# A two-layer encoder step: norms after w_out taken chunk by chunk, GpSimd scaling one chunk, and four seams between stages re-ordered

## The reference

```
mod = silu(c) @ w_ada + b_ada            # six vectors: shift, scale, gate, twice
h = rms_norm(x, g_pre_mix) * (1 + sc1) + sh1
q_s, k_s, v_s, q_f, k_f, v_f, f = split(h @ w_in)
o = concat(window_attention(rope(q_s), rope(k_s), v_s, sinks),
           forgetting_attention(q_f, k_f, v_f, cumsum(log_sigmoid(f))))
x = x + gt1 * rms_norm(o @ w_out, g_post_mix)
h = rms_norm(x, g_pre_mlp) * (1 + sc2) + sh2
u = square(relu(h @ w_up))               # 4096 wide
x = x + gt2 * rms_norm(u @ w_down, g_post_mlp)
```

## Time and profile before

| | |
|---|---|
| profiled execution, device time | 2996.36 us |
| its span of work | 2994.0 us |
| TensorE busy | 2778.9 us (93%) |
| VectorE busy | 1207.7 us (40%) |
| ScalarE busy | 893.3 us (30%) |
| GpSimd busy | 80.3 us (3%) |
| chain that ended last | TensorE 85%, VectorE 7%, ScalarE 3%, transfers 3%, issue 2% |

### The profile page before, as it was taken

The page is one execution under the profiler, slowest core; times in us unless marked ns, Lnnn a source line. Parts: engine busy times, 40 slices in busy tenths (PEclk is TensorE's granted clock), DMA queues, the critical chain, the costliest instruction groups (busy, mean ns, idle before and its releaser), DMA issues.

```text
span 2994.0 us, 45563 instructions
## 1 busy us (share of the span) xinstructions
PE 2778.9 (93%) x18807; PEld 2543.2 (85%) x18807; DVE 1207.7 (40%) x2117; ACT 893.3 (30%) x1711; POOL 80.3 (3%) x50
## 2 busy tenths in 40 slices
PE   4999889896999999999969988999969999999997
PEld 3999666594999999999859985766959999999996
DVE  3214747307433333333450257561183333333335
ACT  4222747324221111221231236562241122111222
POOL 0000300000000000000000003000000000000000
PEclk7999989797999999999979999898979999999998
DMA  8110621221111111111341116121211111111121
GB/s 282 49 64 19 200 65 38 72 87 72 57 42 42 42 56 42 42 42 43 139 153 57 47 59 205 30 57 39 106 68 56 42 42 42 56 42 42 42 78 67
DMA packets 158367, 211.48 MB, mean 71 GB/s; under 512 B 8864, under 2 KB 131792, under 8 KB 157712
## 3 DMA queue, kind: packets, MB, share of 16 engines
q1 hardware_dynamic: 158240, 209.66, 21.1%
HBM read 170.45 MB, written 31.00 MB: 67 GB/s over the span
## 4 chain that ended last, share of the span: by engine, by line
PE 85%; DVE 7%; ACT 3%; DMA 3%; issue 2%; SPq 0%; ACTq 0%; DVEq 0%
PE ps L1385 24%; PE ps L1387 23%; PE ps L1386 23%; PE ps L1678 2%; DVE th L1013 1%; PE ps L1431 1%; PE ps L1630 1%; PE ps L1660 1%; PE ps L1438 1%; DVE st L1196 1%; DMA raw<-w_in 1%; DMA ada_w<-w_ada 1%; PE ps L1573 1%; PE ps L1631 1%; DVE xr L1035 1%
## 5 line engine op out<-in xcount | busy, mean ns | idle before, releaser
L1385 PE MATMUL ps<-hh,wh 128*128 128x352 f32 x2304 | 760.8, 330 | 49.6 <-DVE hl L1021 34.1
L1387 PE MATMUL ps<-hh,wl 128*128 128x352 f32 x2304 | 750.6, 326 | 0.0
L1386 PE MATMUL ps<-hl,wh 128*128 128x352 f32 x2304 | 749.2, 325 | 0.0
L1385 PE MATMUL ps<-uh,wh 128*128 128x352 f32 x1536 | 500.2, 326 | 1.4 <-ACT r_t L934 1.4
L1386 PE MATMUL ps<-ul,wh 128*128 128x352 f32 x1536 | 493.7, 321 | 0.0
L1387 PE MATMUL ps<-uh,wl 128*128 128x352 f32 x1536 | 493.5, 321 | 0.0
L1385 PEld LDWEIGHTS ps<-hh,wh 128*128 128x128 f32 x2304 | 440.7, 191 | 57.4 <-issue 30.5
L1386 PEld LDWEIGHTS ps<-hl,wh 128*128 128x128 f32 x2304 | 442.4, 192 | 0.4
L1387 PEld LDWEIGHTS ps<-hh,wl 128*128 128x128 f32 x2304 | 440.7, 191 | 0.0
L1363 DVE TENSOR_TENSOR y<-ps,y 128x352 f32<-128x352 f32 x384 | 198.1, 523 | 426.3 <-PE ps L1387 426.2
L557 ACT ACTIVATE wh<-raw 128x2048 fp32r<-128x2048 f32 (+1 forms) x90 | 172.0, 1912 | 585.6 <-PE ps L1780 573.7
(11 more groups left out here) (231 smaller groups left out, 3010.8 us busy)
## 6 DMA issues: line engine op xcount, KB each, us to landing
ada_v<-w_ada SPq DMA_DIRECT2D x32, 1024.0 KB, 5.3
raw<-w_up SPq DMA_DIRECT2D x32, 1024.0 KB, 5.3
raw<-w_down SPq DMA_DIRECT2D x32, 1024.0 KB, 4.8
x_kept<-xr SPq DMA_DIRECT2D x12, 1408.0 KB, 8.9
ada_w<-w_ada SPq DMA_DIRECT2D x16, 1024.0 KB, 9.1
...
```

The costliest lines, as they stand in the source:

```text
L1385: pe.matmul(out, w_hi, m_hi, start=start and k == 0, stop=False)
L1386: pe.matmul(out, w_hi, m_lo, start=False, stop=False)
L1387: return pe.matmul(out, w_lo, m_hi, start=False, stop=stop and k == nk - 1)
```

## The change

The same sums are computed, some with their factors in another order. What changes is the order of the lists and who does what, at four places of each layer.

*Norms and MLP.* The norm's work on a chunk is cut from its place behind w_out and set among the groups of round 1 and of the first MLP step, which is written out apart from the loop over the other steps (`first`). A chunk now goes through scale, add, square, factor and affine step before the next begins, and the first MLP step takes its w_up groups chunk by chunk, four per chunk. `pre_rms` and `pre_affine` become `scaled` (x times coefficient times factor, one pass) and a second pass on two engines: ScalarE adds the shift and rounds (`affine_hi`), VectorE adds it and subtracts the rounded half (`affine_lo`). The result goes to a buffer of its own, `tn`. `mean` and `mean_of_parts` stand between the 12th and 13th matmul of a group, or behind one. GpSimd scales chunk 1 of y in place of VectorE, and its fill of y comes after the last `affine_lo`.

*Forgetting attention's beginning.* The last two window steps come ahead of the first two scores groups, the 64 small matmuls of `mod_columns` are set in eights before the scores of x = 0 to 7, and SyncE loads the first score rows one weight block earlier.

*w_out's beginning.* `new_scores` is ahead of w_out and goes over the four heads of a set in turn, its transposes and products one group earlier; ScalarE and VectorE split the first weights earlier.

*In-projection.* VectorE's split of the next weights goes behind the next unit's first rope, and the first block of window queries is rounded within the last unit, into a buffer of its own (`sqh0`).

The diff, cut to its core. GpSimd and SyncE, and the table of the norms' order:

```diff
+                cs = slice(CH, 2 * CH)
+                pool.wait_ge(sm("rb_ok"), idx + 1)
+                pool.tensor_tensor(y[:, :, cs], y[:, :, cs], rb[idx % 2][:, None, :].broadcast_to([P, KT, CH]), ALU.mult).then_inc(sm("y_pool"), 1)
...
-                    if b == 13:
+                    if b == 12:
...
+        NORMS = [(NPRE1, 0), (NPRE1, 1), (NPRE1, 2), (NPOST1, 0), (NPRE2, 0), (NPOST1, 1), (NPOST1, 2), (NPRE2, 1), (NPRE2, 2),
+                 (NPOST2, 0), (NPOST2, 1), (NPOST2, 2)]
```

ScalarE:

```diff
+            def affine_hi(l, c):
...
+                    for k in range(4 * hf, 4 * hf + 4):
+                        for (c0, c1, s_) in stream_pieces(c):
+                            ins = act.activation(hh[:, k, c0:c1], tn[:, k, c0:c1], ACT.Identity, bias=mod[:, 24 + k, s_:s_ + 1])
+                    ins.then_inc(sm("h_hi"), 1)
...
+                        if u == N_TM - 1 and i == 6:
+                            q_hi(0)
...
-                    if w == 15:
-                        expo(0)
+                expo(0)
...
+                    if x == 65:
...
                         split_hi(l, W_WO0)
+                        new_evac()
...
-                split_hi(l, W_WO0 + 1)
...
+                                split_hi(l, W_WO0 + 1)
...
+                        if r == 1 and q == 7:
+                            pre_sq(l, NPRE2, 0)
...
-                        if r == 1 and q % 4 == 3:
-                            post_sq(l, NPOST1, c, l * 24 + 12)
...
+                        if r == 1:
+                            if q in (3, 7):
+                                post_sq(l, NPOST1, c, l * 24 + 12)
+                            if q == 4:
+                                norm_rb(l, NPOST1, 0)
+                            if q == 7:
+                                norm_rb(l, NPRE2, 0)
+                            if q == 8:
+                                affine_hi(l, 0)
+                                norm_rb(l, NPOST1, 1)
+                            if q == 9:
+                                split_hi(l, W_MLP0)
...
-                    split(1)
+                    if not first:
+                        split(1)
...
+                        if first and q == 4:
+                            affine_hi(l, 2)
...
+                            if q == 0:
+                                pre_sq(l, NPRE2, 1)
+                                norm_rb(l, NPOST1, 2)
+                            if q == 1:
+                                norm_rb(l, NPRE2, 1)
+                            if q == 2:
+                                affine_hi(l, 1)
+                            if q == 3:
+                                pre_sq(l, NPRE2, 2)
+                                norm_rb(l, NPRE2, 2)
```

VectorE:

```diff
+            def scaled(l, c):
...
+                            ins = dve.scalar_tensor_tensor(out=tn[:, k, c0:c1], in0=xr[:, k, c0:c1], scalar=coef[:, 2, k, s_:s_ + 1],
+                                                           in1=rb[idx % 2][:, c0 - c * CH:c1 - c * CH], op0=ALU.mult, op1=ALU.mult)
+                    ins.then_inc(sm("nt_ok" if hf else "h_full"), 1)
...
+            def affine_lo(l, c):
...
+                dve.wait_ge(sm(f"x_saved{c}"), (l * 2 + 2) * 16)
...
+                    for k in range(4 * hf, 4 * hf + 4):
+                        for (c0, c1, s_) in stream_pieces(c):
+                            ins = dve.scalar_tensor_tensor(out=hl[:, k, c0:c1], in0=tn[:, k, c0:c1], scalar=mod[:, 24 + k, s_:s_ + 1],
+                                                           in1=hh[:, k, c0:c1].bitcast(F32), op0=ALU.add, op1=ALU.subtract)
...
+                ins.then_inc(sm("h_ok"), 1)
...
+                if by_pool:
+                    dve.wait_ge(sm("y_pool"), 2 * l + 1)
...
-                    if ends(q) and n_of(it) + 2 < W_WO0:
+                    if ends(q) and u < U_GATE and n_of(it) + 2 < W_WO0:
                         split_lo(l, n_of(it) + 2)
+                    if u > U_GATE and i == 0 and n_of(it) + 1 < W_WO0:
+                        split_lo(l, n_of(it) + 1)
...
+                    if u == N_TM - 1 and i == 7:
+                        q_lo(0)
...
+                    if x == 66:
+                        split_lo(l, W_WO0)
...
-                    if x == 69:
-                        split_lo(l, W_WO0)
...
-                split_lo(l, W_WO0 + 1)
...
+                split_lo(l, W_WO0 + 1)
...
-                post_norm(l, NPOST1, 0)
-                post_norm(l, NPOST1, 1)
-                post_norm(l, NPOST1, 2)
-                pre_rms(l, NPRE2, 0)
-                pre_affine(l, NPRE2, 0)
+                post_scale(l, NPOST1, 0)
+                post_add(l, NPOST1, 0)
+                scaled(l, 0)
+                affine_lo(l, 0)
                 split_lo(l, W_MLP0)
-                pre_lo(l, NPRE2, 0)
-                pre_rms(l, NPRE2, 1)
...
+                            if q == 0:
+                                post_scale(l, NPOST1, 2)
+                            if q == 1:
+                                scaled(l, 1)
+                            if q == 2:
+                                affine_lo(l, 1)
+                            if q == 3:
+                                post_add(l, NPOST1, 2)
...
+                        if first and q == 3:
+                            scaled(l, 2)
+                            affine_lo(l, 2)
```

TensorE:

```diff
+                s_tail(15)
+                s_tail(16)
                 scores(0)
-                s_tail(15)
                 scores(1)
-                s_tail(16)
-                pe.wait_ge(sm("so_lo"), (l + 1) * 16)
-                for b in range(16):
-                    ins = mod_columns(ps[:, 7, 4 * b:4 * b + 4], mrow[b // 8][:, (b % 8) * 256:(b % 8 + 1) * 256])
-                ins.then_inc(sm("mod_mm"), 1)
...
+                        outs = [ps[32 * hd:32 * hd + 32, A_BANK[w], 0:W] for hd in range(4)]
...
+                        for h, out in zip(heads, outs):
...
+                            ins = pe.matmul(out, aqs[r, (0 if w < 2 else 4) + h // 2, :], kst[r, w, :] if w < 2 else kft[r, h // 2, :],
...
+                        if w >= 2:
+                            for h, out in zip(heads, outs):
+                                pe.matmul(out, ident[0:NH_F, h:h + 1].broadcast_to([NH_F, NEW]), fsn[:, :], start=False, stop=False,
+                                          skip_group_check=True)
...
+                    if x < 8:
+                        if x == 0:
+                            pe.wait_ge(sm("so_lo"), (l + 1) * 16)
+                        for b in (2 * x, 2 * x + 1):
+                            ins = mod_columns(ps[:, 7, 4 * b:4 * b + 4], mrow[b // 8][:, (b % 8) * 256:(b % 8 + 1) * 256])
+                        if x == 7:
+                            ins.then_inc(sm("mod_mm"), 1)
...
+                new_scores()
...
+                            if r == 1 and k == 4:
+                                if q == 5:
+                                    mean_of_parts(l, NPOST1, 0)
+                                if q == 8:
+                                    mean(l, NPRE2, 0)
+                                if q == 9:
+                                    mean(l, NPOST1, 1)
...
-                                new_scores()
+                            if 1 <= q < 5:
+                                new_transposes(q - 1)
...
-                free_slots(7, 2)
-                mean(l, NPOST1, 2)
-                mean_of_parts(l, NPOST1, 2)
-                for c in range(NCH):
-                    mean(l, NPRE2, c)
-                    mean_of_parts(l, NPRE2, c)
...
+                        if r == 1:
+                            if q == 4:
+                                mean(l, NPOST1, 0)
+                            if q == 8:
+                                mean_of_parts(l, NPRE2, 0)
+                            if q == 9:
+                                free_slots(7)
+                                mean_of_parts(l, NPOST1, 1)
+                            if q == 11:
+                                free_slots(7)
...
+                        if q in ((0, 2) if first else (0, 6)):
...
+                        if first and q % 4 == 0:
                             pe.wait_ge(sm("h_ok"), l * 6 + 4 + c)
...
+                                if q == 1:
+                                    mean(l, NPOST1, 2)
+                                if q == 2:
+                                    mean_of_parts(l, NPRE2, 1)
+                                if q == 5:
+                                    mean(l, NPRE2, 2)
                             ins = step(W_MLP0 + b, ps[:, q % 4, 0:CH], b, j, slice(c * CH, (c + 1) * CH), k, KT, hh, hl)
...
+                        if first:
+                            if q == 1:
+                                mean_of_parts(l, NPOST1, 2)
+                                mean(l, NPRE2, 1)
+                            if q == 5:
+                                mean_of_parts(l, NPRE2, 2)
```

274 lines of the change are left out of this document (147 added, 127 removed).

## The result

The changed kernel takes 2879.41 us (median of four runs, 2872.48 to 2886.38) against 2996.07: a ratio of 0.9613 with a 95% interval of 0.9581 to 0.9645. Forecast were 2891, between 2855 and 2940. The four runs are two pairs, 2885.58 and 2886.38, and 2873.24 and 2872.48, with a granted clock of 0.964 to 0.965 and of 0.969; what makes the pairs is the first thing the experiments ask. So 2879 lies between two groups, and no execution took it. The profiled execution is the 2885.58 one, with a span of 2883.8.

The account below looks back on a forecast made before the run. TensorE, busy 93% of the span, was taken as the bound, so gains come from its gaps or low clock. A 4.8, B 11.8, C 17.1 and D 18.3 make 52.0 a layer, 104 for two: 2891 us, range 2855 to 2940.

Parts of the forecast that it names:

- A: In-projection: two TensorE waits shrink, 2.8 for a rope and 2.0 for window queries; 4.8 us gained per layer.
- B: Beginning of the forgetting attention: waits and the spreading block go, some cost returns; 11.8 us per layer, bounds 0.5 and 18.
- in the midst of big matmuls I count them at full clock: Forgetting attention's beginning: spreading matmuls set among big ones cost 0.40 a block, 16 x 0.40 = 6.4 us.
- Rival (1): The clock stays up at the seams: B 16, C 24, D 21, with A 65.8 per layer; 2864 us, chance 0.20.
- C: Beginning of w_out: earlier weight split and new_scores ahead of w_out; 17.1 us gained per layer, bounds 4 and 24.
- one group earlier I count 1.0: In w_out: the sample's products, waited for behind group 8, come one group earlier and gain 1.0 us.
- Rival (2): The heads of new_scores don't overlap in this form, so C is 3.6; 2918 us, chance 0.13.
- D: Norms between w_out and the MLP: 126.8 us becomes 108.5, with four waits left; 18.3 gained per layer, bounds 8 and 24.
- GpSimd has some 3 to spare: Norms, chunk 1: GpSimd's scale takes 5.2 us, leaving some 3 before TensorE takes the mean behind group u1.
- the 0.7 put down for the collision: Norms: 0.7 us lost because GpSimd and VectorE take turns, around the split of the MLP's first weights.
- Rival (3): GpSimd's scale beside a busy VectorE takes three times as long, 16 us, costing 7.4 a layer; 2906 us, chance 0.15.
- rival (5): Slower: small matmuls put into groups bring the clock to 1.2 GHz over the stretch, and it stays; 3014 us, chance 0.02.

Follow-up runs that it names:

- no_mod: The changed kernel with 15 of the 16 blocks of spreading matmuls (mod_columns) left out; 2867.83 us.
- heads_serial: The changed kernel with new_scores going head by head, each head's four matmuls in a row, as before the change; 2934.47 us in one execution.
- combined: The changed kernel with four edits: sample's copies before w_out's split, VectorE scaling the second chunk, one sum of parts moved, affine_lo reporting half chunks; 2852.97 us.

## Why the prediction was right, step by step

- **A** (4.8): 4.9 in layer 0, with 2.8 and 2.0 for the two waits. Right. In layer 1 the 6.9 hold more: before the change the clock was also at half for 3.4 us behind the wait for the rope (0.57 from 1723 to 1727).
- **B** (11.8): the removed waits went as said, and the new one came, shorter in layer 0 and split in two in layer 1. The step that failed is "in the midst of big matmuls I count them at full clock". It holds in a layer without a fall, 16.1, where the pieces also cost 3 to 4 and not 6.4; with a fall B gains 2 to 3. Rival (1) had the one case. The other lies within B's low bound of 0.5, but no rival has its way: a half clock of some 30 us that the pieces themselves hold on, shown by no_mod. The rows had a hint: at 410 to 416 the clock was still down behind the block of the same matmuls.
- **C** (17.1): 24.2. The wait for ScalarE was 4.95 for 5.2, the scores 7.3 for 9.0, the two groups 9.4 for 10.2. Behind that, "one group earlier I count 1.0" was right for the wait it names, for the sample's products: 1.1. But 5.4 were gained between the second eviction and round 1's group 3, and for the rest the forecast has no term. I had read past it: these products too go over two heads in turn. Before, one head of the third set took 0.42 and 0.30:

```profile
615.92 0.42 PE L1754 MATMUL ps<-apt,cvf 128*64 128x32 f32 x4
616.27 0.30 PE L1755 MATMUL ps<-apt,vf 32*64 32x32 f32 x2
616.50 0.42 PE L1754 MATMUL ps<-apt,cvf 128*64 128x32 f32 x4
```

and after, two heads take as long:

```profile
584.87 0.42 PE L1863 MATMUL ps<-apt,cvf 128*64 128x32 f32 x8
585.22 0.30 PE L1863 MATMUL ps<-apt,vf 32*64 32x32 f32 x4
```

So each of the four sets takes half: 0.92, 0.92, 1.15 and 1.15 less, 4.1 together. This is read from the rows; no run takes it apart. Rival (2) is ruled out by heads_serial. Rival (1)'s C of 24 was reached by another way than its own: new_scores ran at half clock, and only in combined at full clock, in 4.1.
- **D** (18.3): 15.9 and 17.8. The chains held to a tenth in two waits (2.28 and 4.50) and to half a us in a third (5.07 for 4.6). What failed is "GpSimd has some 3 to spare" and the estimate of 5.2 under it: the operation took 6.3, 2.24 ns an element where the one of the earlier trace rows takes 1.85 (whether by its size or by its operand `rb`, which is repeated over the row blocks, isn't shown), and the 0.7 put down for the collision was 2.1 at TensorE. The chain of chunk 2 then had its 2.9 covered by TensorE's own lateness, so the sum of the waits, 14.0, came out as forecast by two errors of opposite sign. The low clock and the semaphores behind the waits, 2.6 and 1.0 in the forecast, were 6.9 and 4.5 together: 110.9 and 108.9 less 90.1 and less 14.0 and 14.3. The windows at half clock account for nearly all of it in layer 0 (1.7, 3.0 and 2.2 lost), so next to nothing is left over for a price of the means' places in the midst of groups.
- Rival (3), GpSimd at three times its price, and rival (5) did not come: in the changed kernel's D the clock fell only behind waits of over 2 us, not among the means.
